# Cached keys of a hybrid attention step: TensorE transposes against pieces of 32 floats and block transposes on VectorE

## What is computed

```python
k_all = jnp.concatenate([c_fk.astype(fk.dtype), fk], axis=1)     # cached keys: 8 batches x 512 tokens x 8 heads x 64
s = jnp.einsum('bqhd,bkhd->bhqk', q, k).astype(jnp.float32) * FOX_SCALE
s = s + jnp.swapaxes(cum_q, 1, 2)[..., :, None] - jnp.swapaxes(cum_k, 1, 2)[..., None, :]
pr = jax.nn.softmax(jnp.where(mask, s, NEG_INF), axis=-1)
return jnp.einsum('bhqk,bkhd->bqhd', pr.astype(v.dtype), v)
```

## Time and profile before

| | |
|---|---|
| median of 3 runs | 1526.13 us (1526.04 to 1526.81) |
| the profiled execution: its own time | 1525.61 us |
| its span, first to last instruction | 1523.7 us |
| mean granted TensorE clock | 0.986 |
| TensorE busy | 1466.4 us, 96% of the span |
| VectorE busy | 552.8 us, 36% |
| ScalarE busy | 313.2 us, 21% |
| DMA | 483.48 MB, 317 GB/s over the span |
| sample loop | 176.8 to 284.4 us |
| expert stage | from about 584 us |

### The profile page before, as it was taken

One profiled execution on the slowest core, in us unless ns is written; L12 is line 12 of the kernel. 1 busy time (PEld: TensorE's weight loads), 2 busy tenths in 40 slices (PEclk: granted clock), 3 DMA queues, 4 the chain that ended last, 5 costly groups with the idle time before them and its releaser, 6 DMA issues.

```text
span 1523.7 us, 21869 instructions
## 1 busy us (share of the span) xinstructions
PE 1466.4 (96%) x8246; PEld 719.8 (47%) x8247; DVE 552.8 (36%) x1240; ACT 313.2 (21%) x676; POOL 45.4 (3%) x55
## 2 busy tenths in 40 slices
PE   8999899999999998999999999999999999999996
PEld 7766577655687653333333333333333333333332
DVE  4245444110302465343343333343333433433334
ACT  1225555210001441111111111111111111111111
POOL 0000000160000000000000000000000000000000
PEclk9999999999999998999999999999999999999998
DMA  9421466942332468999999999999999999999994
GB/s 286 131 67 46 116 184 214 306 153 87 111 125 83 152 262 360 428 427 428 429 428 428 428 429 428 428 428 386 429 429 428 429 428 428 428 429 428 428 428 197
DMA packets 83038, 483.48 MB, mean 317 GB/s; under 512 B 18145, under 2 KB 46081, under 8 KB 56369
## 3 DMA queue, kind: packets, MB, share of 16 engines
q1 hardware_dynamic: 68800, 471.78, 75.7%
q0 software_dynamic: 3168, 9.11, 2.6%
q10 hardware_dynamic: 11024, 1.96, 0.8%
HBM read 475.16 MB, written 4.65 MB: 315 GB/s over the span
## 4 chain that ended last, share of the span: by engine, by line
PE 79%; DMA 16%; DVE 2%; issue 1%; ACT 1%; SPq 0%; DVEq 0%; ACTq 0%
PE bank L529 73%; DMA ring<-in_w_gu 16%; PE bank L1278 1%; PE bank L683 1%; PE bank L1203 1%; DMA ring<-in_w_in 1%; PE bank L920 0%; PE bank L806 0%; PE bank L694 0%; PE bank L1066 0%; DVE small L1661 0%; PE bank L543 0%; DVE ring L1672 0%; PE bank L961 0%; DVE xr L1982 0%
## 5 line engine op out<-in xcount | busy, mean ns | idle before, releaser
L529 PE MATMUL bank<-ring,hT 128*64 128x512 f32 (+3 forms) x3648 | 813.9, 566 | 15.4 <-DMA ring<-in_w_gu 14.6
L529 PEld LDWEIGHTS bank<-ring,hT 128*64 128x64 f32 (+1 forms) x3648 | 305.6, 145 | 439.3 <-issue 387.2
L1940 DVE SCALAR_TENSOR_TENSOR xr<-bank,probTs,xr 128x512 f32<-128x512 f32 x198 | 139.3, 745 | 231.7 <-PE bank L529 231.7
L529 PE MATMUL bank<-hT,ring 128*128 128x384 f32 x384 | 124.4, 486 | 0.0
L2329 ACT ACTIVATE probTs<-hT 128x512 f32<-128x512 f32 x33 | 20.8, 631 | 441.5 <-DVE hT L1959 441.5
L1977 DVE TENSOR_TENSOR mlaT<-bank,foxT 128x512 f32<-128x512 f32 x33 | 22.8, 692 | 224.5 <-ACT foxT L2335 224.5
L529 PEld LDWEIGHTS bank<-hT,ring 128*128 128x128 f32 x384 | 72.8, 190 | 50.3 <-issue 0.2
L529 PE MATMUL bank<-ring 128*128 128x256 f32 (+7 forms) x434 | 84.6, 394 | 4.0 <-issue 2.5
L529 PE MATMUL bank<-foxT 64*128 64x512 bf16 x600 | 82.1, 379 | 0.8 <-ACT foxT L2335 0.8
L529 PEld LDWEIGHTS bank<-ring 128*128 128x128 f32 (+3 forms) x434 | 58.7, 170 | 20.2 <-issue 11.5
L2335 ACT CAST foxT<-bank 128x512 bf16<-128x512 f32 x33 | 19.3, 585 | 215.7 <-PE bank L529 215.7
(11 more groups left out here) (330 smaller groups left out, 1274.6 us busy)
## 6 DMA issues: line engine op xcount, KB each, us to landing
ring<-in_w_gu SPq DMA_DIRECT2D x128, 2048.0 KB, 24.4
ring<-in_w_down SPq DMA_DIRECT2D x64, 2048.0 KB, 26.8
ring<-in_w_in SPq DMA_DIRECT2D x16, 1024.0 KB, 11.3
ring<-in_cache_fox_k SPq DMA_DIRECT2D x8, 1024.0 KB, 4.8
ring<-in_cache_fox_v SPq DMA_DIRECT2D x8, 1024.0 KB, 7.7
ring<-in_cache_mla_ckv SPq DMA_DIRECT2D x8, 512.0 KB, 5.6
ring<-in_w_out SPq DMA_DIRECT2D x4, 1024.0 KB, 5.1
ring<-in_cache_mem_k SPq DMA_DIRECT2D x8, 512.0 KB, 3.3
```

The costliest lines, as they stand in the source:

```text
L529: return pe.matmul(o, l, r, start=start, stop=stop, skip_group_check=True)
L1940: v.scalar_tensor_tensor(x, sums[i % 2][:, :], gate_e[:, i // 2, e], x, ALU.mult, ALU.add).then_inc(shares_added, 1)
```

## The change

Seven batches, all but batch 5, take another way (`FINE`). Their keys are loaded by 16 DMAs each (`key_tile`): one for each of four groups of 128 numbers and each of four bands of 32 partitions. A DMA takes 512 pieces of 32 floats (128 bytes) and lays them so that 32x32 blocks stand in the slot. VectorE then turns these blocks: four instructions of 128x512 a batch (`keys_in`), written with a scattered pattern so that `skT` holds what it held before. TensorE waits for a count of turned batches (`keys_turned`) in `sample_scores`; its transposes for these batches, and the copies out of their banks on both engines, are gone. Batch 5 goes the old way.

Two orders change with it. In `stream`, the keys of batch b + 1 stand ahead of the latents of batch b. In TensorE's pass, the first latent group of batch b + 1 is turned ahead of the fox values, the second one and the rotary keys where all stood. A slot that held fine keys is released by `keys_turned`.

```diff
+FINE = (0, 1, 2, 3, 4, 6, 7)
+        def key_tile(b):
+            if b not in FINE:
+                tile(("sk", b), whole(KT, FW, d["cache_fox_k"][0, b].rearrange("(p k) h n -> p k (h n)", k=KT)))
+                return
+            src = d["cache_fox_k"][0, b].rearrange("(i r) (g e) (f c) -> g e f r i c", r=32, e=2, c=32)
+            parts = []
+            for g in range(4):
+                for j in range(4):
+                    parts.append((lambda s, g=g, j=j: ring[32 * j:32 * j + 32, s, FW * g:FW * g + FW].rearrange("p (i c) -> p i c", c=32),
+                                  src[g, j // 2, j % 2, :, :, :]))
+            tile(("sk", b), parts)
+
+        key_tile(0)
         for b in range(NB):
-            tile(("sk", b), whole(KT, FW, d["cache_fox_k"][0, b].rearrange("(p k) h n -> p k (h n)", k=KT)))
+            if b + 1 < NB:
+                key_tile(b + 1)
             tile(("sc", b), [(lambda s: kview(s, KT, LORA), d["cache_mla_ckv"][0, b].rearrange("(p k) n -> p k n", k=KT)),
...
             def turn_keys(b, pairs):
+                if b in FINE:
+                    return
...
-            def turn_latents(b):
+            def turn_latents(b, parts=(0, 1)):
                 s = arrived(pe, ("sc", b))
                 c3 = kview(s, KT, LORA)
-                for c in range(2):
+                for c in parts:
...
+                if 1 not in parts:
+                    return
                 ps = open_bank(pe, ("srT", b))
...
             def sample_scores(b):
...
-                for g in range(4):
-                    pe.wait_ge(free(("skT", b, g)), count(("skT", b, g)))
+                if b in FINE:
+                    pe.wait_ge(keys_turned, FINE.index(b) + 1)
+                else:
+                    for g in range(4):
+                        pe.wait_ge(free(("skT", b, g)), count(("skT", b, g)))
...
                 if b + 1 < NB:
                     turn_keys(b + 1, (0, 1))
+                    turn_latents(b + 1, (0,))
                 if b >= 1:
                     sample_values(2 * b - 2)
                 if b + 1 < NB:
                     turn_keys(b + 1, (2, 3))
-                    turn_latents(b + 1)
+                    turn_latents(b + 1, (1,))
...
-                if n >= NRING:
-                    g = last_group[stream[n - NRING][0]]
+                before = stream[n - NRING][0]
+                if n >= NRING and before[0] == "sk" and before[1] in FINE:
+                    sp.wait_ge(keys_turned, FINE.index(before[1]) + 1)
+                elif n >= NRING:
+                    g = last_group[before]
                     sp.wait_ge(bank_full[g % 8], g // 8 + 1)
...
+            def keys_in(b):
+                if b in FINE:
+                    key = ("sk", b)
+                    dve.wait_ge(ring_loaded[slot(key)], loaded_at[place[key]])
+                    for g in range(4):
+                        last = v.transpose(skT[b % 2][:, g, :].rearrange("p (k i q) -> p i q k", k=KT, q=8), ring[:, slot(key), FW * g:FW * g + FW])
+                    last.then_inc(keys_turned, 1)
+                else:
+                    for g in range(2):
+                        copy_out(("skT", b, g), skT[b % 2][:, g, :])
...
                 if i == 7:
                     dve.wait_ge(fk_written, 32)
-                    for g in range(2):
-                        copy_out(("skT", 0, g), skT[0][:, g, :])
+                    keys_in(0)
...
             def cache_out(b):
                 if b >= 2:
                     dve.wait_ge(full(("sS", 2 * b - 3)), count(("sS", 2 * b - 3)))
-                for g in range(2):
-                    copy_out(("skT", b, g), skT[b % 2][:, g, :])
+                keys_in(b)
                 copy_out(("scT", b, 0), scT[b % 2][:, 0, :])
...
-                for g in range(2, 4):
-                    copy_out(("skT", b, g), skT[b % 2][:, g, :])
+                if b not in FINE:
+                    for g in range(2, 4):
+                        copy_out(("skT", b, g), skT[b % 2][:, g, :])
```

More of the change, by code:

```diff
@@ L319, in build @@
         krope_ready = sem("krope_ready")
+        keys_turned = sem("keys_turned")
         ckv_ready = sem("ckv_ready")
```

## The result

The changed kernel takes 1569.91 us (1567.23 to 1570.97, four runs), the kernel before, beside it, 1526.47: a ratio of 1.0285 (1.0273 to 1.0297). It is slower, as forecast, but by 43.4 us instead of 10, and the time lies outside the range. Its profiled execution took 1569.21 us.

What follows compares the result with a forecast made beforehand. TensorE, always busy in the sample loop, was taken as the bound there. Latent waits +10.05, clock +3.9, relieved passes -4.32, pass 0 +0.4 and ahead of the loop +0.3 gave +10.3 us: 1536, range 1519 to 1548.

Steps and rivals of the forecast that it cites:

- 3r - 26.6: Forecast sum in us without the clock's term; r is when the latents or rotary keys land in the pass, taken as 11.0.
- Part 4: Keys loaded in pieces by 16 DMAs on SyncE: 7.7 us a batch; latents behind them land at 11.0 instead of 6.07.
- The upper bound in the sum: Longest time for a batch's 8192 pieces, from the rate of a shared queue: 14.1 us.
- rival C: DMA engines brake the pieces: 14.1 us a batch, landing at 17.4, +29.5 us, 1555; chance 0.11.
- Landing behind the issues: Rotary keys behind the pieces land 3.0 us after issue, as on a quiet queue; bound 5.4.
- Part 2: Four block transposes on VectorE, 0.65 us each; hidden in steady passes, +0.3 us before the loop, +0.4 in pass 0.
- rival D: Slow block transposes on VectorE, 1.3 us each: +5.3 us on the forecast, 1541.7; chance 0.10.
- Pass 1: TensorE's loop pass without key transposes, forecast to gain 1.44 us like passes 3 and 6.
- the clock's term: TensorE's clock falls after each of three waits for latents: 1.3 us each, 3.9 us; bounds 0 and 2.0 each.
- Ahead of the loop: VectorE's block transposes stand ahead of probabilities that TensorE awaits before the loop: +0.3 us.
- the relieved passes: Loop passes without TensorE's key transposes and undisturbed last 12.03 us, 1.44 us less.
- the one-for-one path to the end: Everything behind the sample loop is released by it, so its gain or loss carries to the end in full.

Runs made afterwards that it cites:

- the last experiment: Changed kernel with fine keys only for batches 2, 3, 4, 6, latents ahead of keys, bias of 4 and 6 after their pieces: 1526.58 us, ratio 1.0001.

## Why the prediction was wrong in size

The mechanism was forecast: passes 2, 4 and 5 wait for rotary keys behind sixteen issues, passes 3 and 6 gain, and a lower clock follows the waits. By the prediction's own formula the measured landings, 18.9, 18.7 and 17.8 us into the pass, give 3r - 26.6 = 55.4 - 26.6 = 28.8 instead of 6.4. That is 22.4 of the 33.5 us between forecast and result. Only the executions with a profile are taken apart here. Step by step:

**Part 4, the sixteen issues: the step that failed.** The term was 7.7 us; ahead of the loop it is 8.31, an acceptable miss, but in the loop 13.7 to 14.6. I had put the bias spread at 0.75 us, by its bytes at the full rate, while the earlier trace rows gave 8.9 us for it from issue to landing. Beside pieces it takes no longer:

```profile
ring<-xr POOLq DMA_DIRECT2D x1, 320.0 KB, 8.3
```

That row is from 211 to 220 us of the kernel after, in the middle of the pieces: the pieces are slowed by the bias, and not it by them. Moving it away gave 8.3 to 9.4 us. The Trainium skill ("DMA: Bandwidth & Descriptors", Queues, rings and completion order) says that a DMA engine takes turns between its queues packet by packet, a packet holding several descriptors, typically 9 to 17; by that rule an engine's pieces stand still while it moves a packet of the bias, and some of them go between two. The two DMA views agree as far as they go: fewer pieces at an unchanged cost each, 2958 for 59 packets of the bias as the profile counts them. The turns themselves no view here shows: that the spread slows the issues is shown, how it does so is not.

The upper bound in the sum, 14.1 us from a mixed stretch, was the size that came. I gave it to rival C, where the pieces themselves are dear, and let C out of the range because "nothing but the bias shares in the loop". C's landing, 17.4, was nearly met, and its cause, packets well over 13 ns, was not. The same bound should have stood in the forecast's own range, since that stretch held a second queue with 2700 packets on the same engines, just as the loop has the bias. That 14.1 met the 13.7 to 14.6 so closely is luck: the second queue there was another.

**Landing behind the issues.** 3.0 us was taken from a quiet queue; 3.7 to 4.0 came (222.27 to 226.15). That is 0.9 us a wait.

**Part 2, the block transposes.** 0.65 us was taken, 0.92 came, within the bounds, though over the 0.7 us named as the sign of rival D. The copy's row gave the instruction without its scatter nearly to the point (0.62). The estimate from the Trainium skill's 311 ns ("VectorE: DVE Perf Modes", The three transpose paths), 1.24 us, is above both. Pass 0 followed the working exactly: VectorE is free for batch 1 at 185.82, 3.02 us later than before, as the loop is, and four transposes end when pass 1 starts.

```profile
185.82 3.68 DVE L1715 STREAM_TRANSPOSE ring<-ring 128x512 f32<-128x512 f32 x4
```

So +1.33 instead of +0.4 there. In steady passes they stay hidden, as said: no later pass waits for VectorE.

**Pass 1.** It was to gain 1.44 us and lost 4.23: 5.7 us that the clock took. Stretches of the kernel after, columns as in rows 2:

```profile
190.00:195.00 5.00, 5.00 (x25) 2.71 (x18) 2.82 (x14) 0.97 (x4) 0.00 (x0) 0.50 0.75 207
195.00:200.00 5.00, 5.00 (x11) 1.93 (x10) 0.00 (x0) 0.20 (x3) 0.59 (x1) 0.50 0.41 58
200.00:205.00 5.00, 5.00 (x63) 4.16 (x61) 4.77 (x10) 3.38 (x12) 0.00 (x0) 0.76 0.27 31
```

TensorE stood 3.63 us for VectorE and then worked without a gap at 0.50, 1.2 instead of 2.4 GHz, for ten microseconds. I had read just this behind a wait of 3.69 us, but put it into the sum only after the waits for latents. That pass 0 ends in a wait was in my own part 2 (its transposes gone, TensorE has nothing to do until 2.6 us of VectorE are over); the clock's term was not applied to it. That a transpose took longer than forecast doesn't excuse it: in the kernel without the scatter the wait was 2.42 us and pass 1 still took 15.0 us.

**The clock after the three long waits.** 1.3 us each was taken; the rest of passes 2, 4 and 5 took 7.25, 7.94 and 7.76 us for 5.51, 6.44 and 5.51: 1.7, 1.5 and 2.3, the last a little over the bound of 2.0.

**Ahead of the loop.** +0.3 was forecast and +3.02 measured. About 1.5 of that doesn't seem to be the change's: four of the kernels here with the same loads up to that point issue batch 2's pieces at 128.7 to 128.9 us, this execution at 130.32. The kernel with batches 0, 1 and 5 the old way, at 130.38 as late, starts its loop 1.2 us behind the kernel before with the same wait of 3.68 us. Where this delay comes from stays open. The rest, some 1.5 us, comes with the transposes ahead of the prompt's probabilities: that wait is 7.05 us in place of 3.69, and 5.90 without the scatter.

**Right:** the relieved passes, 12.10 us where 12.03 was worked out (in pass 3 the second value product starts 8.87 us into the pass, as said, and the rest takes 3.23 for 3.16); ScalarE's copies at no cost; pieces at 12.75 ns (12.7); and the one-for-one path to the end (43.8 in the loop, 43.7 in the span).

The gap sums up: landings 22.4, pass 1 5.7, ahead of the loop 2.7, clock 1.6, pass 0 0.9: 33.3 of 33.5 us.

## What to carry to other kernels

Many small transfers on a queue cost what lies behind them in that queue, so list each deadline there and keep the pieces where nothing that is due soon follows: here, ahead of the loop. Size a transfer that shares the DMA engines by its own time from issue to landing in the trace, not by its bytes at the full rate; one slow spread nearly doubled the time of sixteen quick issues beside it. Apply the clock's price to every wait of TensorE that a change makes, not only to the large ones: 3.6 us of waiting cost 3 to 6 us more behind it, and 2.00 us in the last experiment some 1.4, while the 0.79 us in the kernel with two fine batches cost no more than itself.

## What the runs showed of the hardware that was not expected

The scatter of a block transpose has a price: 0.62 us for 128x512 written side by side, 0.92 to 0.96 us with its four-byte elements strewn.

A broadcast of 320 KB takes 8.3 us to land beside pieces and 8.9 beside large loads, while the issue of sixteen DMAs of 512 pieces goes from 8.3 us to 13.7 to 14.6 beside it (15.48 beside three transfers of GpSimd), though a piece holds a DMA engine for 12.7 ns in both cases.

How long the clock stays low after the same wait differs. With pass 1's wait at 3.62 or 3.63 us, that pass took 17.7 us in the kernel after and in those with the bias later and with half of the pieces, and 15.0 in those with the late batches the old way and with the latents first. With the late batches the old way the first five microseconds hold the same work at the same clock as in the kernel after, but in the second five the mean clock is 0.89 (columns as above):

```profile
189.00:194.00 5.00, 5.00 (x25) 2.71 (x18) 2.81 (x14) 0.97 (x4) 0.00 (x0) 0.50 0.76 209
194.00:199.00 5.00, 4.97 (x45) 2.78 (x46) 1.60 (x6) 1.33 (x5) 0.59 (x1) 0.89 0.40 56
```

Why the clock came back earlier there stays open; the runs don't tell it apart.
